# Reversing the k-steps of the middle token tile in the x-fed panels of a two-layer streaming encoder

## The chip, the cores and the metric

The kernel runs on one core of one Trainium2 chip. The metric is the device time of one execution, in microseconds (us). Before the change, three runs took 2115.74, 2115.85 and 2116.09 us, so the median is 2115.85 us. One further execution was profiled, and every row quoted here comes from it.

## The reference, cut to what matters

The model is one inference step of a two-layer encoder trunk over 1056 token rows (1024 of a prompt and 32 of a running stream), each with 1024 features. Each layer is a mixer and then a squared-ReLU MLP, with an RMS norm before and after each. In short:

```python
for l in range(2):
    hn = rmsnorm(x, norm_mix_pre[l])
    m = mixer_even(hn, ...) if l == 0 else mixer_odd(hn, ...)   # hn @ w_in first, w_out last
    x = x + rmsnorm(m, norm_mix_post[l])
    hn = rmsnorm(x, norm_ffn_pre[l])
    f = square(relu(hn @ mlp_up[l])) @ mlp_down[l]              # 1024 -> 4096 -> 1024
    x = x + rmsnorm(f, norm_ffn_post[l])
```

Four matrix products read the normed x: `w_in_even` (1024 to 2048 features), `mlp_up` of layer 0 (1024 to 4096), `c_w_in` (1024 to 3072) and `mlp_up` of layer 1. The change touches only these four. Each output feature is a sum over the 1024 input features. The kernel forms it in eight parts of 128, which are the k-steps, and they may be added in any order.

## The kernel before

**Data.** Features lie on the 128 partitions and tokens along the free dimension. The 1056 tokens are cut into three tiles of 352 columns, t = 0, 1, 2. Every fp32 operand of a product is kept as two rounded parts, high and low: `x_hi` and `x_lo` hold the normed x in eight feature chunks, and `h_hi` and `h_lo` hold the inner activations. A weight panel holds the 1024 x 128 weights of one output chunk, also as a high and a low part.

**Units.** `plan()` (line 79) writes down 736 units of TensorE work in the order in which they run. A whole unit is one panel times one tile. It consists of eight k-steps, and each k-step of three matmuls: weights high times data high (line 881), weights high times data low (line 882), and weights low times data high (line 883). That makes 24 matmuls of 352 columns into one PSUM bank. The first has `start`, the last has `stop` and increments the semaphore `pe_unit` (line 885). The bank is the unit's number modulo six. A unit that reads x is marked `src == "X"`. The 280 remaining units that are not whole are Strassen products of the MLP's down projection (lines 927 to 930), each with 12 matmuls of 264 columns.

**Phases.** `START` holds the first units of the four phases that read x: 0, 72, 356 and 452. The first twelve units of a phase are a block of four panels, tile by tile, and the semaphore `x_ready` is waited for only in units 0, 4 and 8 of a phase, once for each k-step (lines 875 and 876). After that block, a panel goes through its three tiles in a row: 0, 1, 2, or 2, 1, 0 for the third and fourth panel of a Strassen group's up projection (line 159). Phase 0 has 12 panels after its block, phases 1 and 3 have 28 each and phase 2 has 20.

**What sets the order around it.** `unit(n)` (line 863) waits once for all of its panel (`w_ready`, line 870) and once for its bank (line 871). It then issues the k-steps by `order`. `between(n, i)` (line 1060) inserts small matmuls after step number i of certain units, by position in the loop and not by k. The panels' transfers go out from SyncE (line 653), each after the last unit that reads the panel's slot (`pe_unit`). ScalarE makes the high part of the weights (line 1116). VectorE makes the low part and empties the banks after whole units (lines 1635 and 1678, for instance).

Of the kernel before, what the change touches and what calls it, by code (L numbers as in the profile page):

```python
# [205 lines left out]
def build(nc, A, O):  # L206
    UNITS, LOADS, START, OUT, GROUP = plan()
# [67 lines left out]
    with ExitStack() as ctx:  # L275
# [102 lines left out]
        def pt(buf, c, t):  # L378
            c0 = c * (buf.shape[1] // KC) + tile_at(buf, t)
            return buf[:, c0:c0 + TT]  # L380
# [36 lines left out]
        def w_k(l, which, k):  # L417
            v = W[l][which]
            if LOADS[l].slot in ("ha", "hb"):
                return v[:, k // 2, (k % 2) * P:(k % 2) * P + P]  # L420
            return v[:, k, :]
# [10 lines left out]
        def bank(n):  # L432
            return ps[:, R[n] % NB, 0:TT]
# [425 lines left out]
        def _(pe):  # L859
# [3 lines left out]
            def unit(n):  # L863
                u = UNITS[n]
                X = u.src == "X"
                src = (x_hi, x_lo) if X else (h_hi, h_lo)
                order = EVEN_ORDER if u.kind == "eo" else IN_ORDER[0:SC] if u.kind == "dn0" else IN_ORDER
                w0 = SC * (u.m % 2) if u.kind == "dn0" else 0
                l, t = u.load, u.t
                pe.wait_ge(w_ready, l + 1)  # L870
                bank_free(n)
                phase = START.index(max(s for s in START if s <= n))
                dst = bank(n)
                for i, k in enumerate(order):
                    if X and n - START[phase] in (0, 4, 8):
                        pe.wait_ge(x_ready, 24 * phase + 8 * t + k + 1)
                    if u.m == 0:
                        h_part(n, i)
                    hi, lo = pt(src[0], k, t), pt(src[1], k, t)
                    wh, wl = w_k(l, 0, w0 + k), w_k(l, 1, w0 + k)  # L880
                    nc.tensor.matmul(dst, wh, hi, start=(i == 0), stop=False)  # L881
                    nc.tensor.matmul(dst, wh, lo, start=False, stop=False)  # L882
                    last = nc.tensor.matmul(dst, wl, hi, start=False, stop=(i == len(order) - 1))  # L883
                    if i == len(order) - 1:
                        last.then_inc(pe_unit, 1)
                    between(n, i)

            def bank_free(n):
                o = bank_user[n]
                if o is not None:  # L890
                    pe.wait_ge(evac_a if UNITS[o].kind in SCALAR_OUT else evac_d, evac_no[o] + 1)
# [69 lines left out]
            def h_part(n, i):  # L961

                kind, t = UNITS[n].kind, UNITS[n].t
                if kind == "dn0" and i == 0:
                    pe.wait_ge(h_ready, index[n - 1 - t] + 1 - 8 + 4 * t)
                if kind == "dn3":
                    done = index[n - 1 - t] + 1
                    if i == 0 and t == 0:
                        pe.wait_ge(h_ready, done - 3)
                    if i == KC - 1:  # L970
                        pe.wait_ge(h_ready, done - 2 + t)
                if kind == "oo":
                    if i == 0 and t == 0:
                        pe.wait_ge(y_ready, 21)
                    if i == KC - 1:
                        pe.wait_ge(y_ready, 22 + t)
                if kind == "eo":
                    if i == 0 and t == 0:
                        pe.wait_ge(mix_a, 12)
                    if i == 4 and t == 0:  # L980
                        pe.wait_ge(mix_a, 21)
                    if i == KC - 1:
                        pe.wait_ge(mix_a, 22 + t)
# [76 lines left out]
            def between(n, i):  # L1060

                if n < START[1]:
                    if (n, i) in GATE_AT:
                        gate(*GATE_AT[n, i])
                    if (n, i) in VALUE_AT:
                        values_to_rows(*VALUE_AT[n, i])
                    if (n, i) in SPATIAL_AT:
                        spatial(SPATIAL_AT[n, i])
                if (n, i) in COL_AT:
                    col_sums(*COL_AT[n, i])  # L1070
# [10 lines left out]
            for n in range(4, N_UNITS):  # L1081
                if UNITS[n].kind in STRASSEN:
                    product(n)
                else:
                    unit(n)
# [7 lines left out]
            n = NORM[3, "post", 2]  # L1093
# [951 lines left out]
```

## Time and profile before

| what | value |
|---|---|
| median of three runs | 2115.85 us |
| the profiled execution's own time | 2116.21 us |
| its span, first to last instruction | 2114.1 us |
| mean granted TensorE clock | 0.999 of full |
| TensorE matmul busy | 2105.2 us, 100% |
| TensorE weight load busy | 2094.1 us, 99% |
| VectorE busy | 1187.2 us, 56% |
| ScalarE busy | 718.6 us, 34% |
| GpSimd busy | 279.3 us, 13% |

The profiled execution took 2.1 us more than its span. Busy time of matmuls is counted with overlap taken out, and each matmul's record is longer than the distance to the next one's start, so a busy TensorE is not one at its peak. For its pace one reads the distances between start times.

### The profile page before, as it was taken

What the parts mean: (1) busy time and instruction counts of PE and PEld (TensorE: products, weight loads), DVE (VectorE), ACT (ScalarE), POOL (GpSimd) and SP (SyncE); (2) the same over time, 40 slices, a digit from 0 to 9 for tenths busy, and PEclk for the clock granted to TensorE, in tenths of its full rate; (3) what the DMA queues carried; (4) which work ended last, traced back from release to release, by engine and by line L of the source; (5) the groups of instructions that cost most, each with busy time, mean ns of one, the idle gap of its engine ahead of it and who ended that gap; (6) DMA issues with size and microseconds to landing.
All of it is one profiled execution on the core that took longest, in us unless ns stands there. A gap on an engine that the chain in (4) does not pass through costs nothing.

```text
span 2114.1 us, 33629 instructions
## 1 busy us (share of the span) xinstructions
PE 2105.2 (100%) x13976; PEld 2094.1 (99%) x13976; DVE 1187.2 (56%) x1798; ACT 718.6 (34%) x1225; POOL 279.3 (13%) x307
## 2 busy tenths in 40 slices
PE   9999999999999999999999999999999999999998
PEld 9999999999999999999999999999999999999998
DVE  8766367364755747334953333384566475564336
ACT  6673345132232322333511112352313233232332
POOL 2000000031221312000033232000113022130000
PEclk9999999999999999999999999999999999999999
DMA  4111422111111111141311114131111111111142
GB/s 165 39 38 40 137 78 85 51 51 42 51 48 51 51 51 51 42 141 40 123 51 40 51 50 133 41 122 51 45 52 45 51 51 51 51 51 46 46 142 82
DMA packets 209189, 138.78 MB, mean 66 GB/s; under 512 B 6768, under 2 KB 205552, under 8 KB 209040
## 3 DMA queue, kind: packets, MB, share of 16 engines
q1 hardware_dynamic: 208320, 135.51, 21.1%
q8 instruction: 112, 1.84, 0.4%
q10 hardware_dynamic: 720, 1.13, 0.1%
q14 instruction: 37, 0.30, 0.0%
HBM read 119.22 MB, written 17.40 MB: 65 GB/s over the span
## 4 chain that ended last, share of the span: by engine, by line
PE 89%; issue 10%; DMA 0%; POOL 0%; DVE 0%; DVEq 0%; ACTq 0%; SPq 0%; POOLq 0%
PE ps L881 23%; PE ps L882 23%; PE ps L883 23%; PE ps L927 6%; PE ps L929 6%; PE ps L930 6%; PE ps L1003 1%; PE ps L1031 0%; PE ps L957 0%; PE ps L948 0%; DMA w_all_raw<-in_w_in_even_dram 0%; PE ps L944 0%; DMA w_all_raw<-in_mlp_down_dram 0%; PE ps L1014 0%; PE ps L990 0%
## 5 line engine op out<-in xcount | busy, mean ns | idle before, releaser
L881 PE MATMUL ps<-x_hi,w_all 128*128 128x352 f32 x2304 | 751.4, 326 | 0.0
L883 PE MATMUL ps<-x_hi,w_all 128*128 128x352 f32 x2304 | 739.4, 321 | 0.0
L882 PE MATMUL ps<-x_lo,w_all 128*128 128x352 f32 x2304 | 739.3, 321 | 0.0
L882 PEld LDWEIGHTS ps<-x_lo,w_all 128*128 128x128 f32 x2304 | 433.6, 188 | 2.2
L881 PEld LDWEIGHTS ps<-x_hi,w_all 128*128 128x128 f32 x2304 | 432.6, 188 | 2.7
L883 PEld LDWEIGHTS ps<-x_hi,w_all 128*128 128x128 f32 x2304 | 432.3, 188 | 0.0
L1116 ACT CAST w_all<-w_all_raw 128x1024 fp32r<-128x1024 f32 (+1 forms) x166 | 199.8, 1204 | 422.0 <-DMA w_all_raw<-in_mlp_up_dram 167.6
L927 PE MATMUL ps<-h_hi,w_all 128*128 128x264 f32 x1120 | 318.9, 285 | 0.0
L929 PE MATMUL ps<-h_lo,w_all 128*128 128x264 f32 x1120 | 318.6, 284 | 0.0
L930 PE MATMUL ps<-h_hi,w_all 128*128 128x264 f32 x1120 | 318.0, 284 | 0.0
L1635 DVE SCALAR_TENSOR_TENSOR tmp<-ps,rstd 128x352 f32<-128x352 f32 x192 | 100.1, 522 | 284.6 <-PE ps L883 284.5
L1643 DVE TENSOR_TENSOR f<-ps,f 128x528 f32<-128x528 f32 x280 | 195.7, 704 | 108.2 <-PE ps L930 107.8
L881 PE MATMUL ps<-h_hi,w_all 128*128 128x352 f32 x768 | 248.9, 324 | 0.0
L882 PE MATMUL ps<-h_lo,w_all 128*128 128x352 f32 x768 | 246.4, 321 | 0.0
L883 PE MATMUL ps<-h_hi,w_all 128*128 128x352 f32 x768 | 246.3, 321 | 0.0
L929 PEld LDWEIGHTS ps<-h_lo,w_all 128*128 128x128 f32 x1120 | 211.0, 188 | 0.0
L927 PEld LDWEIGHTS ps<-h_hi,w_all 128*128 128x128 f32 x1120 | 210.9, 188 | 0.0
L930 PEld LDWEIGHTS ps<-h_hi,w_all 128*128 128x128 f32 x1120 | 210.9, 188 | 0.0
L1466 DVE TENSOR_TENSOR w_all<-w_all_raw,w_all 128x1024 fp32r<-128x1024 f32 x126 | 153.8, 1221 | 17.6 <-ACT w_all L1116 17.6
L788 POOL TENSOR_TENSOR h_lo<-h_lo_raw,h_hi 128x528 fp32r<-128x528 f32 x20 | 26.5, 1325 | 972.7 <-ACT h_hi L1197 972.7
L881 PEld LDWEIGHTS ps<-h_hi,w_all 128*128 128x128 f32 x768 | 144.2, 188 | 0.3 <-DVE h_lo L1806 0.3
L882 PEld LDWEIGHTS ps<-h_lo,w_all 128*128 128x128 f32 x768 | 144.5, 188 | 0.0
(225 smaller groups left out, 2415.5 us busy)
## 6 DMA issues: line engine op xcount, KB each, us to landing
w_all_raw<-in_mlp_up_dram SPq DMA_DIRECT2D x60, 512.0 KB, 3.9
w_all_raw<-in_mlp_down_dram SPq DMA_DIRECT2D x96, 256.0 KB, 3.1
x_save<-f SPq DMA_DIRECT2D x9, 1408.0 KB, 6.5
x_old<-x_save SPq DMA_DIRECT2D x9, 1408.0 KB, 11.7
w_all_raw<-in_c_w_in_dram SPq DMA_DIRECT2D x22, 512.0 KB, 3.6
w_all_raw<-in_w_in_even_dram SPq DMA_DIRECT2D x12, 512.0 KB, 3.6
w_all_raw<-in_mlp_down_dram SPq DMA_DIRECT2D x12, 512.0 KB, 4.0
x_old<-in_x_cols_dram SPq DMA_DIRECT2D x3, 1408.0 KB, 11.2
```

The costliest lines, as they stand in the source:

```text
L788: nc.gpsimd.tensor_tensor(t_form(h_lo, 1, c), raw, t_form(h_hi, 1, c).bitcast(F32), ALU.subtract).then_inc(t1_ready, 1)
L881: nc.tensor.matmul(dst, wh, hi, start=(i == 0), stop=False)
L882: nc.tensor.matmul(dst, wh, lo, start=False, stop=False)
L883: last = nc.tensor.matmul(dst, wl, hi, start=False, stop=(i == len(order) - 1))
L927: nc.tensor.matmul(dst, wh, hi, start=(c == 0 and u.kind in CHAIN_START), stop=False, skip_group_check=True)
L929: nc.tensor.matmul(dst, wh, lo, start=False, stop=False, skip_group_check=True)
L930: last = nc.tensor.matmul(dst, wl, hi, start=False, stop=(c == 1), skip_group_check=True)
L1003: nc.tensor.matmul(ps[:, M0, 0:LT], gate_w[:, g, j, :], xc[j % 2][:, t * LT:(t + 1) * LT], start=True, stop=True).then_inc(gate_pe, 1)
L1116: nc.scalar.copy(W[l][0], W[l][2]).then_inc(w_high, 1)
L1466: nc.vector.tensor_tensor(lo, raw, hi.bitcast(F32), ALU.subtract).then_inc(w_ready, 1)
L1635: ins = nc.vector.scalar_tensor_tensor(sq_tmp(n)[:, :], bank(n), 0.0, scale, ALU.max, ALU.mult)
L1643: ins = nc.vector.tensor_tensor(sums, ps[:, a:a + 2, 0:QT], sums, ALU.add)
```

## The change

Inside `unit(n)`, for a unit that reads x, has t = 1 and is at least the thirteenth of its phase, the order of the eight k-steps is turned round: 7, 6, ... 0 in place of 0, 1, ... 7. The three matmuls inside a k-step keep their order. Nothing else is edited.

```diff
@@ -871,6 +871,8 @@
                 bank_free(n)
                 phase = START.index(max(s for s in START if s <= n))
                 dst = bank(n)
+                if X and t % 2 == 1 and n - START[phase] > 11:
+                    order = order[::-1]
                 for i, k in enumerate(order):
                     if X and n - START[phase] in (0, 4, 8):
                         pe.wait_ge(x_ready, 24 * phase + 8 * t + k + 1)
```

## Rows read from the trace of the kernel before

**Rows 1.** The page: its head, and busy time of each engine.

```profile
span 2114.1 us, 33629 instructions
PE 2105.2 (100%) x13976; PEld 2094.1 (99%) x13976; DVE 1187.2 (56%) x1798; ACT 718.6 (34%) x1225; POOL 279.3 (13%) x307
```

**Rows 2.** The page: 40 slices of the span, matmuls and granted clock, in tenths.

```profile
PE   9999999999999999999999999999999999999998
PEclk9999999999999999999999999999999999999999
```

**Rows 3.** Waits of TensorE matmuls (PE), then weight loads (PEld): us, times, longest us.

```profile
PE ps L1040 <- DVE rstd L1693: 1.3, 1, 1.3
PE ps L1048 <- ACT x_old L1453: 0.3, 1, 0.3
...
PEld ps L881 <- DVE h_lo L1806: 0.3, 1, 0.3
```

**Rows 4.** Line 881, by operands: count, duration ns min/median/max, first and last start.

```profile
L881 PEld LDWEIGHTS ps<-x_hi,w_all x2304: 186/188/193, 22.9 to 2009.5; 128*128 128x128 f32 x192
L881 PE MATMUL ps<-x_hi,w_all x2304: 317/323/597, 23.1 to 2009.7; 128*128 128x352 f32 x192
...
L881 PE MATMUL ps<-x_hi,h_hi x144: 320/323/409, 313.1 to 1430.5; 128*128 128x352 f32 x144
...
L881 PE MATMUL ps<-x_hi,w_s x16: 322/323/594, 34.8 to 56.0; 128*128 128x352 f32 x16
```

**Rows 5.** Timeline of matmuls, with the first of five units, after 492 us: start, duration (us).

```profile
492.37 0.28 PE L930 MATMUL ps<-h_hi,w_all 128*128 128x264 f32 x1
492.48 0.33 PE L881 MATMUL ps<-x_hi,w_all 128*128 128x352 f32 x1
...
496.36 0.32 PE L881 MATMUL ps<-x_hi,w_all 128*128 128x352 f32 x1
...
500.21 0.32 PE L881 MATMUL ps<-x_hi,w_all 128*128 128x352 f32 x1
...
511.49 0.32 PE L883 MATMUL ps<-x_hi,w_all 128*128 128x352 f32 x1
511.65 0.32 PE L881 MATMUL ps<-x_hi,w_all 128*128 128x352 f32 x1
511.81 0.32 PE L882 MATMUL ps<-x_lo,w_all 128*128 128x352 f32 x1
511.97 0.32 PE L883 MATMUL ps<-x_hi,w_all 128*128 128x352 f32 x1
...
515.47 0.32 PE L881 MATMUL ps<-x_hi,w_all 128*128 128x352 f32 x1
...
530.73 0.32 PE L881 MATMUL ps<-x_hi,w_all 128*128 128x352 f32 x1
```

**Rows 6.** Timeline of weight loads around 511.6 us: start, duration (us).

```profile
511.50 0.19 PEld L881 LDWEIGHTS ps<-x_hi,w_all 128*128 128x128 f32 x1
511.65 0.19 PEld L882 LDWEIGHTS ps<-x_lo,w_all 128*128 128x128 f32 x1
```

**Rows 7.** Two windows, Strassen products then x units: busy us and instructions of each engine.

```profile
455.00:490.00 35.00, 35.00 (x290) 35.00 (x289) 24.68 (x37) 6.42 (x6) 9.31 (x10) 1.00 0.16 46
500.20:538.35 38.15, 38.15 (x242) 38.15 (x241) 21.69 (x32) 16.06 (x32) 8.40 (x8) 1.00 0.15 42
```

**Rows 8.** Waits of VectorE and of SyncE's queue for TensorE: us, times, longest us.

```profile
DVE tmp L1635 <- PE ps L883: 284.5, 140, 3.3
...
SPq L669 <- PE ps L883: 803.7, 79, 17.5
```

## The prediction

> **What bounds the kernel.** I read the page's head first: the span is 2114.1 us and matmuls are busy for 2105.2 us of it [rows 1]. Then the slices, to see whether a stretch differs: all but the last have TensorE at nine tenths or more, and its clock is granted nearly in full throughout [rows 2]. Then the waits: in the whole execution TensorE's matmuls waited 1.6 us for other engines, once at the start and once in the tail, and the largest wait of a weight load at line 881 is 0.3 us [rows 3]. So no semaphore holds TensorE, and the kernel is a stream of 13976 matmuls. Its time can change only if the distance between the starts of two matmuls changes, if the number of matmuls changes, or if a new wait arises.
>
> The timeline gives that distance. The units that begin at 500.21 and 530.73 us are eight apart, so 192 matmuls took 30.52 us, 158.96 ns each [rows 5]. One unit of 24 matmuls takes 3.815 us. The records last 0.32 us, twice the distance, since a matmul's record goes on while the next has begun.
>
> **What the change removes, adds and moves.** It reverses the middle unit of each panel that comes after a phase's first twelve units: 12 panels in phase 0, 28 in phase 1, 20 in phase 2 and 28 in phase 3, together 88 units. That is 88 x 8 = 704 of the 2464 k-steps at line 881 that read x (2304 + 144 + 16, [rows 4]), and 88 x 24 = 2112 matmuls of 13976. No instruction goes or comes. What changes is which chunk of x and which block of weights a k-step reads. I take the possible costs one by one.
>
> *Waits on inputs.* The wait for `x_ready` stands only in units 0, 4 and 8 of a phase, and these are not reversed. By the thirteenth unit every chunk of every tile has been waited for. The wait for the weights covers a whole panel and was passed in the panel's first unit, which is never the middle one. So step 7, now first, needs nothing that is not there. Cost 0, covered by waits already passed.
>
> *Who waits for the unit.* VectorE empties a bank after the unit's last matmul; it waits 284.5 us in 140 cases at line 1635 for exactly that. SyncE's queue waits for the same count before a transfer, 803.7 us in 79 cases at line 669 [rows 8]. Both count whole units. The last matmul still stands at the end, whatever its k. No transfer starts earlier or later, and no queue is passed by a moved step: the k-steps issue no DMA. The small matmuls of phase 0 and the column sums are inserted by position. Cost 0. If a unit did end later, the cover is gone only for TensorE itself, and that is the case priced as the slow rival below.
>
> *Weight loads.* One could hope that a k-step which stays at k = 7 from tile 0 to tile 1, and at k = 0 from tile 1 to tile 2, saves a load. It would have to be of the same weights. But a k-step ends with the low weights (line 883) and the next begins with the high ones (line 881), so the two neighbours differ there too. And where neighbours do have equal weights, lines 881 and 882 in every k-step, the trace still has a load for each: 13976 loads for 13976 matmuls [rows 1], one at 511.50 and one at 511.65 us, 0.19 us each [rows 6]. The pair with equal weights is 0.16 us apart (511.65 to 511.81), and so is the pair with different ones (511.81 to 511.97) [rows 5]. So nothing is saved in the number of loads, and a saved load would show no gain in distance anyway. Value taken: 0.
>
> *The hops.* The reversal changes two kinds of steps from one matmul to the next. At the two edges of each reversed unit the hop becomes a stay on the same chunk, 2 x 88 = 176 hops. Inside it, a step up by one chunk becomes a step down by one, 7 x 88 = 616 hops. Together 792. The trace before has no step down by one, but it has larger ones: at each tile edge TensorE goes from chunk 7 back to chunk 0. The edge from tile 1 to 2 at 511.65 us is 0.16 us wide, as are its neighbours [rows 5]. Single distances are too coarse, so I compare whole units. From 500.21 to 515.47 us four units run through tiles 2, 0, 1, 2, that is with tile edges mostly upwards; it is 15.26 us. From 515.47 to 530.73 us four units run through tiles 2, 1, 0 and then 2 of the next panel, with edges downwards; it is 15.26 us again [rows 5]. The tile hop has changed direction and nothing is left of it at 0.01 us over four units, or 2.5 ns a unit. Put down to the two edges of a unit, that is 1.25 ns a hop. For 792 hops this bounds the cost to 792 x 1.25 = 1.0 us on either side. I take 0, since the nearest rows, the large backward hops, show no difference.
>
> *A wider bound from the pace itself.* A matmul's time has a part that follows its columns and a part that doesn't. In 35.00 us of Strassen products there are 290 matmul records of 264 columns, of which about two were in flight at the edge, so 35.00/288 = 121.5 ns each [rows 7]. Against 158.96 ns for 352 columns the slope is 37.4/88 = 0.425 ns a column. Of the 158.96 ns, 352 x 0.425 = 149.7 follow the columns and 9.3 are fixed. If hop or order were the cause of the fixed part, at most 2112 x 9.3 = 19.6 us could go. Against it speaks that the fixed part is the same whether the weights stay or change.
> The Trainium skill (TensorE: Matmul & The Clock Gate, section "Wait — 56ns, not 53.3ns?") gives the start-to-start distance at full clock as columns over 2.4 GHz plus about 2.5 ns. By that page alone it would be 149.2 ns here, an estimate. The trace disagrees: 158.96 ns. Were the reversed units to run at the page's pace, 2112 x 9.8 = 20.7 us would go. The page's rule has no term for the order of k, so it gives no reason why they should.
>
> **The sum.** Waits 0, loads 0, hops 0 with ends of -1.0 and +1.0 us. The profiled execution stays at a span of 2114.1 us and a time of 2116.2 us. That is 0.36 us above the median of the three runs, well within what one run differs from another (2115.74 to 2116.09 us). The forecast for the median is therefore 2115.85 us. About 0.2%, or 4.2 us, is what a measurement of this kernel can tell from no change.
>
> **The rivals.**
> *An edge that stays on a chunk is cheaper.* TensorE reads the same weight block and adjoining columns of x across the edge, and the whole fixed part of 9.3 ns goes at 176 hops: 1.6 us, 2114.2 us. For it: the operands are neighbours in memory. Against it: lines 881 and 882 share their weight block in every k-step and show no shorter distance [rows 5].
> *The fixed part goes in all of the reversed units.* 19.6 us, 2096.3 us. It needs a cause that sits in the direction of the steps inside a unit. For it is only that no row shows a step down by one; against it are the equal unit times for both directions of the tile edge.
> *Slower: reversed units lose the pace of the stream.* There is a slower pace in this trace: the units at 492.48 and 496.36 us, directly behind a Strassen group, take 3.88 and 3.85 us, not 3.815 [rows 5]. TensorE comes there from shorter matmuls, waits for nobody, and regains its pace in two units. If a step down by one chunk upset the fetching of operands ahead in the same way, each reversed unit would cost 0.065 us more, 88 x 0.065 = 5.7 us, or 2121.6 us. It decides from 4.2/88 = 0.048 us a unit, or 2 ns a matmul. Against it: the hops from chunk 7 to chunk 0, seven times as far, do not upset it from 500.21 us on.
> *The change doesn't act.* The reversed order is held in a name local to the unit and is read by the loop right after, so it acts on 88 units. Were it not to, the time would be the same 2115.85 us, and only the order of accumulation would tell.
>
> **How the numbers follow.** Forecast, no change beyond the hops' bound: 0.85. Cheaper edges: 0.07. No action: 0.01. Slow rival: 0.04. Fixed part gone in whole units: 0.03. The first three are within 0.2%, hence 0.93 for the same, 0.03 for faster and 0.04 for slower. The range holds the forecast with the hops' 1.0 us and the 0.4 us that medians may differ, and takes in the cheaper edges: 2114.2 to 2117.3 us. It leaves out the two far cases, 0.07 together.
>
> **What would show it.** In the profile after, the panels' middle units should again be 3.81 or 3.82 us long. The starts should stay at the same places within a tenth of a us to the end, with 13976 matmuls and as many loads, TensorE's waits at about 1.6 us in all, and the waits of VectorE and SyncE's queue for line 883 unchanged in count. The distance across a reversed unit's edges should be 0.16 us. The prediction is wrong if middle units are 0.05 us longer or shorter than the outer ones of the same panel, or if a wait appears before line 881. A change of the span with unchanged middle units would say that the cause is elsewhere and that I have overlooked something which counts k-steps.

## The result, and the profile after

The changed kernel takes 2125.70 us (median of four runs, 2125.50 to 2125.93) against 2115.87 us of the kernel before. The ratio is 1.0046, with a 95% interval of 1.0033 to 1.0059. No change was forecast, and 2114.2 to 2117.3 us as the range. The loss is 9.8 us.

The page's head of the kernel after, to be held against [rows 1]:

```profile
span 2123.9 us, 33629 instructions
PE 2115.1 (100%) x13976; PEld 2104.3 (99%) x13976; DVE 1187.8 (56%) x1798; ACT 718.8 (34%) x1225; POOL 279.4 (13%) x307
```

The counts are the same to the last instruction, and the span and the busy time of TensorE have grown alike, by 9.8 and 9.9 us. Next come the waits of the kernel after: TensorE's own, then VectorE's and that of SyncE's queue for TensorE (us, times, longest us). Line numbers behind the edit are two higher than before.

```profile
PE ps L1042 <- DVE rstd L1695: 1.3, 1, 1.3
PE ps L1050 <- ACT x_old L1455: 0.3, 1, 0.3
...
DVE tmp L1637 <- PE ps L885: 290.5, 140, 3.3
...
SPq L669 <- PE ps L885: 809.3, 79, 17.5
```

TensorE waits for the others for 1.6 us, as before [rows 3]. VectorE and SyncE's queue wait for TensorE as many times as before, and each about 6 us longer in all [rows 8]. So no wait has arisen. TensorE itself runs slower.

Where it does is seen in windows. The first two rows are the kernel before, the last two the kernel after. The columns are: window, its length, then busy us and instructions of PE, PEld, DVE, ACT and POOL, the granted clock, the DMA share and GB/s. The first window is TensorE's work on x panels in phase 2, the other on that phase's output panels.

```profile
1100.00:1290.00 190.00, 190.00 (x1197) 190.00 (x1196) 64.47 (x97) 25.02 (x46) 55.97 (x54) 1.00 0.16 46
1315.00:1380.00 65.00, 65.00 (x411) 65.00 (x411) 25.64 (x33) 26.04 (x48) 0.00 (x0) 1.00 0.25 76
```

```profile
1100.00:1290.00 190.00, 190.00 (x1181) 190.00 (x1180) 62.84 (x95) 26.23 (x49) 54.21 (x54) 1.00 0.16 46
1315.00:1380.00 65.00, 65.00 (x411) 65.00 (x410) 22.93 (x30) 22.44 (x41) 0.00 (x0) 1.00 0.26 85
```

In the same 190 us TensorE does 16 matmuls fewer, at a granted clock of 1.00 in both. (By the lengths of the units below it is 161.1 ns a matmul in place of 158.9; the windows' counts include matmuls cut by their ends.) The output panels, which read h in unchanged order, run at the old pace but for the first two units. This window of 190 us serves below as a yardstick: 1197 matmuls is the fast pace and 1181 the slow one.

Then the timeline of the kernel after, the first matmul of the same units as in [rows 5] (start, duration in us):

```profile
492.59 0.33 PE L883 MATMUL ps<-x_hi,w_all 128*128 128x352 f32 x1
...
496.47 0.33 PE L883 MATMUL ps<-x_hi,w_all 128*128 128x352 f32 x1
...
500.34 0.33 PE L883 MATMUL ps<-x_hi,w_all 128*128 128x352 f32 x1
...
515.80 0.33 PE L883 MATMUL ps<-x_hi,w_all 128*128 128x352 f32 x1
...
531.27 0.33 PE L883 MATMUL ps<-x_hi,w_all 128*128 128x352 f32 x1
```

Before, the first unit behind the Strassen group took 3.88 us, the second 3.85, and from 500.21 us on each took 3.815. After, they take 3.88 and 3.87, and from 500.34 us on it is (531.27 - 500.34)/8 = 3.866 us a unit to the end of the stretch. All three tiles are slow, not only the reversed one. Added up over the x units of phases 1 to 3 that come after a phase's first twelve, the middle tiles lost 3.1 us and the two untouched tiles 6.3 us. TensorE no longer leaves the slow pace that the trace before shows at 492.48 us. It leaves it only in the output panels, whose order is unchanged: behind phase 2 their first unit (at 1305.95 us) takes 3.87 us, the second 3.85 and the third 3.81. And where TensorE comes in fast, nothing is lost: the twelve x units from 405.94 us on take 3.813 us each. They follow units of only four k-steps, 24 in phase 1 and as many in phase 3, which the section on the kernel before counts as whole ones.

### The profile page after: what moved, and what is told of

Read it like the earlier page. It is cut to its first block, busy times and chain, and to the rows that moved or that the text cites. A ratio compares the mean times of both kernels' runs of the same rounds, so it can differ in the third digit from the quotient of the medians.

```text
span 2123.9 us, 33629 instructions
## 1 busy us (share of the span) xinstructions
PE 2115.1 (100%) x13976; PEld 2104.3 (99%) x13976; DVE 1187.8 (56%) x1798; ACT 718.8 (34%) x1225; POOL 279.4 (13%) x307
## 4 chain that ended last, share of the span: by engine, by line
PE 89%; issue 10%; DMA 0%; POOL 0%; DVE 0%; DVEq 0%; ACTq 0%; SPq 0%; POOLq 0%
PE ps L883 23%; PE ps L885 23%; PE ps L884 23%; PE ps L929 6%; PE ps L931 6%; PE ps L932 6%; PE ps L1005 1%; PE ps L1033 0%; PE ps L959 0%; DMA w_all_raw<-in_w_in_even_dram 0%; PE ps L950 0%; PE ps L946 0%; PE ps L1016 0%; DMA w_all_raw<-in_mlp_down_dram 0%; PE ps L992 0%
```

## The experiments

**The theory.** Chunk k of tile t begins (1056k + 352t) x 4 = 128 x (33k + 11t) bytes into x. Whether this is an even or an odd multiple of 128 bytes goes by k + t; call it the parity of a k-step. `x_lo` begins an even number of times 128 bytes behind `x_hi`, so it has the same parity. In steps of one chunk the parity alternates. Before, it was repeated at both edges of a middle unit: k=7,t=0 (odd) to k=0,t=1 (odd), and k=7,t=1 (even) to k=0,t=2 (even). The reversal makes these edges alternate as well. Theory A: a repeat of parity takes TensorE out of a slow pace, and pure alternation keeps it there. Theory B: steps down cost. Theory C: the same weight block on both sides of an edge costs.

**Order and parity apart.** Two kernels, each with one line in place of the change's:

```diff
-                    order = order[::-1]
+                    order = (6, 5, 4, 3, 2, 1, 0, 7)      # e1_down_even
+                    order = (1, 2, 3, 4, 5, 6, 7, 0)      # e2_up_odd
```

> Only the order of the reversed units is another: 6, 5, 4, 3, 2, 1, 0, 7 in all 88. Chunk k of tile t starts 128 x (33k + 11t) bytes into x, so whether it is an even or an odd multiple of 128 bytes goes by k + t (its parity). Before the change the two edges of a middle unit repeat a parity (k=7,t=0 to k=0,t=1, and k=7,t=1 to k=0,t=2); the full reversal lets the parity alternate everywhere. Theory A (the missing repeats leave TensorE in the slower of two paces, 161 instead of 159 ns a matmul): this order starts even and ends odd, so both edges repeat a parity again, hence 2115.9 us. Theory B (each step down by one chunk costs): six of seven inner steps go down still, 2115.9 + 9.8 x 6/7 = 2124.3 us. Theory C (the same weight block on both sides of an edge costs): no edge has it, 2115.9 us.

> The order of the 88 middle units is 1, 2, 3, 4, 5, 6, 7, 0: all steps go up but for the last. Theory A (parity repeats at the edges missing): it starts odd and ends even, no parity is repeated, 2125.7 us, and all three tiles of a panel at 3.867 us. Theory B (steps down cost): 2115.9 us, or 2117 with the single large one. Theory C (same weight block at an edge costs): the edge 7 to 1 is free of it and the edge 0 to 0 has it, half of 9.8 us, 2120.8 us.

The first took 2115.93 us (ratio 1.0000, 0.9991 to 1.0009), the second 2125.70 us (1.0047, 1.0032 to 1.0062). Six of seven steps down cost nothing where the edges repeat a parity. Steps up cost all of the 9.8 us where they don't. The yardstick window, first kernel and then second:

```profile
1100.00:1290.00 190.00, 190.00 (x1197) 190.00 (x1196) 64.48 (x97) 25.04 (x47) 56.04 (x54) 1.00 0.16 46
```

```profile
1100.00:1290.00 190.00, 190.00 (x1181) 190.00 (x1180) 62.86 (x95) 26.19 (x48) 54.09 (x54) 1.00 0.16 45
```

Theory B is refuted by both, theory C by the second, where it expected 2120.8 us.

**Which operand.** The change was applied to one operand alone:

```diff
+                    mid = X and t % 2 == 1 and n - START[phase] > 11
+                    kx = KC - 1 - k if mid else k            # e3_x_only
+                    hi, lo = pt(src[0], kx, t), pt(src[1], kx, t)
...
+                    kw = KC - 1 - k if mid else w0 + k       # e4_w_only
+                    wh, wl = w_k(l, 0, kw), w_k(l, 1, kw)
```

> In the 88 middle units only the chunk of x is reversed, the weight block goes 0 to 7, so the products pair the wrong chunks; number and size of all instructions are as before. Theory A (parity of the addresses of x): 2125.7 us. Theory B (steps down in x): 2125.7 us; if it is steps down in the weights, 2115.9 us. Theory C (same weight block at an edge): 2115.9 us.

> The counterpart: in the 88 middle units only the weight block is reversed, the chunk of x goes 0 to 7, so the products pair the wrong chunks. The blocks of a panel lie 512 bytes apart, so their parity never changes. Theory A (parity of the addresses of x): 2115.9 us. Theory B with steps down in the weights, and theory C: 2125.7 us.

With only x reversed it took 2125.60 us (1.0046, 1.0031 to 1.0061), with only the weights reversed 2115.82 us (1.0000, 0.9990 to 1.0009). It is the order of the addresses of x that matters, not that of the weight blocks. In both kernels the products pair the wrong chunks, so their time alone is used. The weight blocks of a panel are 512 bytes apart and never change parity.

**Does each reversed unit pay, or does the stretch keep a pace?**

```diff
-                if X and t % 2 == 1 and n - START[phase] > 11:
+                if X and t % 2 == 1 and n - START[phase] > 11 and u.m > 0:   # e5_down_later
                     order = order[::-1]
```

> The change as it was, but without the panels with m = 0 (74 units reversed in place of 88). These 14 are nearly all the first x panel behind a Strassen group or behind the phase's block, where TensorE arrives at its slow pace. Theory A with a memory (a pace is kept while the parity alternates, and each repeat of a parity moves TensorE one step from the slow to the fast one): the forward panel repairs the pace (3.879, 3.848, 3.812 us), the reversed ones behind it keep the fast one, 3.813 us a unit in place of 3.813, 3.815 and 3.818. 2115.9 less some 70 panels x 0.007 us = 2115.4 us. Theory A without a memory (each reversed unit pays at its own edges), and any theory in which a reversed unit costs by itself: 2115.9 + 9.8 x 74/88 = 2124.1 us.

It took 2115.48 us (five rounds, 2115.20 to 2115.95; before 2115.85 in the same rounds; ratio 0.9998, 0.9989 to 1.0007). 74 of 88 reversals cost nothing when a forward panel has come before them. The timeline of this kernel, first matmuls of the units as above:

```profile
492.14 0.33 PE L883 MATMUL ps<-x_hi,w_all 128*128 128x352 f32 x1
...
496.02 0.32 PE L883 MATMUL ps<-x_hi,w_all 128*128 128x352 f32 x1
...
499.87 0.32 PE L883 MATMUL ps<-x_hi,w_all 128*128 128x352 f32 x1
...
515.12 0.32 PE L883 MATMUL ps<-x_hi,w_all 128*128 128x352 f32 x1
...
530.37 0.32 PE L883 MATMUL ps<-x_hi,w_all 128*128 128x352 f32 x1
```

The first two units take 3.88 and 3.85 us as in the kernel before, and from 499.87 us on eight units take 30.50 us, 3.813 each. So alternation keeps the fast pace as well as it keeps the slow one.

**Many repeats.** All x units behind the first twelve of a phase took the even chunks first, then the odd ones:

```diff
+                if X and n - START[phase] > 11:
+                    order = (0, 2, 4, 6, 1, 3, 5, 7)      # e6_even_odd
```

> All three tiles of every x panel behind the first twelve units (264 units) take their k-steps as 0, 2, 4, 6, 1, 3, 5, 7: six parity repeats inside a unit. If alternation itself costs and a repeat saves time, the units get shorter than 3.813 us. If a repeat only moves TensorE out of the slow pace and costs 2 to 3 ns at the fast one (3.815 and 3.818 us in units with a repeat, against 3.813 without), it is 264 x 6 x 2.5 ns = 4 us more, 2119 to 2120 us. Theory B (steps down cost) has one step down a unit and expects 2116 us.

2117.39 us (1.0007, 0.9998 to 1.0016). A repeat is not fast by itself. The amount was overestimated: 1.5 us lost in place of 4. A panel of this kernel has 20 repeats and takes 3.820 us a unit in place of 3.813, about 1 ns a repeat and not 2.5. In this trace the first unit behind Strassen takes 3.93 us, and in its first four steps, whose parity is all even, the matmuls stay about 0.167 us apart. That fits what the slow units show inside. In the kernel after, 211 units without small matmuls, all with their weights in the three weight slots, take 3.87 us, and in them every k-step of even parity takes 0.490 us and every one of odd parity 0.476 or 0.477. At the fast pace, with alternating parity, all k-steps take 0.474 to 0.479 us. In e6 a unit at the fast pace takes 3.82 us with its repeats.

**A kick instead of the edges.** All 88 units stay reversed, and twelve first units of a stretch get two repeats inside:

```diff
                     order = order[::-1]
+                if X and (UNITS[n - 1].kind in STRASSEN or n in (START[0] + 12, START[2] + 12)):
+                    order = (0, 1, 3, 2, 4, 5, 6, 7)      # e7_down_kick
+                    order = (0, 1, 3, 2, 5, 4, 6, 7)      # e10_down_kick_apart, in its place
```

> The change as it was, all 88 units reversed, and in addition 12 forward units get the order 0, 1, 3, 2, 4, 5, 6, 7: the first x unit behind each Strassen group, the first behind the block of phase 2 and of phase 0. That order has two repeats (1 to 3, 2 to 4) inside the unit. Theory A with a memory: these twelve units bring TensorE to the fast pace and the reversals keep it there, 3.813 us a unit to the end of the stretch; the whole 9.8 us vanish and some 0.5 us more, about 2115 us. If repeats inside a unit, where the weight block changes parity in nothing, do not work as those at the edges do: 2125.7 us. Any theory in which reversed units cost by themselves: 2125.7 us.

It took 2120.26 us (1.0021, 1.0012 to 1.0029), half of the loss and between the two expectations. The timeline shows why: the second unit and all behind it take 3.84 us.

```profile
496.34 0.32 PE L885 MATMUL ps<-x_hi,w_all 128*128 128x352 f32 x1
...
500.18 0.32 PE L885 MATMUL ps<-x_hi,w_all 128*128 128x352 f32 x1
...
530.90 0.32 PE L885 MATMUL ps<-x_hi,w_all 128*128 128x352 f32 x1
```

From 500.18 to 530.90 us it is 3.840 us a unit. There are three paces, and alternation keeps each. The order had only taken TensorE one step.

Another version rests on the theory in its first form. It reverses only in phases 1 to 3 and has the same kick also in other slow units:

```diff
+                if X and t % 2 == 1 and n - START[phase] > 11 and phase > 0:
+                    order = order[::-1]
+                if X and (UNITS[n - 1].kind in STRASSEN or phase > 0 and n - START[phase] in (2, 10)):
+                    order = (0, 1, 3, 2, 4, 5, 6, 7)
+                if u.kind in ("oo", "dn3", "eo") and (u.m, t) == (5, 2):
+                    order = (4, 5, 7, 6, 0, 1, 2, 3) if u.kind == "eo" else (0, 1, 3, 2, 4, 5, 6, 7)
```

> A version built on theory A to beat both kernels: reversals in phases 1 to 3 only (76 units), the order with two repeats in the first x unit behind a Strassen group, in the third and eleventh unit of the blocks of phases 1 to 3 (3.869 and 3.877 us before, and slow ones behind them), and in the unit with m = 5, t = 2 of the four output blocks (3.867 us). Theory A with a memory: behind Strassen 10 x 0.07, alternation 70 x 0.007, blocks 3 x 0.25, outputs 4 x 0.05 us, together 2.1 us: 2113.8 us. Otherwise at least 2115.9 us, up to 2124.

It took 2119.67 us (1.0018, 1.0009 to 1.0026) and sat at the middle pace as well. In the next two kernels the two repeats are three steps apart. The second of them keeps the forward order where m = 0:

> All 88 units reversed, and the 12 first units with the order 0, 1, 3, 2, 5, 4, 6, 7 in place of 0, 1, 3, 2, 4, 5, 6, 7, which took 2120.3 us since 3.840 us a unit stayed for the whole stretch. If the second repeat had come too early: 3.813 us a unit, 2115 us. If an even repeat inside a unit does nothing at the middle pace: 2120.3 us again. If reversed units cost by themselves: no less than 2120.

```diff
-                    order = (0, 1, 3, 2, 4, 5, 6, 7)                    # e8_best
+                    order = (0, 1, 3, 2, 5, 4, 6, 7)                    # e9_both
...
-                    order = (4, 5, 7, 6, 0, 1, 2, 3) if u.kind == "eo" else (0, 1, 3, 2, 4, 5, 6, 7)
+                    order = (4, 5, 7, 6, 1, 0, 2, 3) if u.kind == "eo" else (0, 1, 3, 2, 5, 4, 6, 7)
```

> The version that reversed 74 units took 2115.48 us; this one reverses its 65 of phases 1 to 3, and gives the first x unit behind each Strassen group, the third and eleventh unit of three blocks and one unit of each output block the order 0, 1, 3, 2, 5, 4, 6, 7. Its two parity repeats (1 to 3, both odd, and 4 to 6, both even) stand three k-steps apart, not one as in 0, 1, 3, 2, 4, which left TensorE on a pace between the two (3.840 us a unit). Theory A with three paces, where a repeat of each parity is wanted with some k-steps between: fast behind each such unit, 2114.1 us (Strassen sites 10 x 0.05, blocks 3 x 0.15, outputs 4 x 0.07, alternation 0.5 us). If an even repeat inside a unit does nothing wherever it stands: blocks and outputs go to the middle pace, the two edges behind Strassen do the rest, 2115.0 us. Neither if theory A is wrong: 2116 us or more.

All 88 reversed with the kick apart: 2115.03 us (0.9996, 0.9987 to 1.0005), where 2115 was expected. The other: 2113.93 us (0.9991, 0.9983 to 1.0000), where 2114.1 was expected. The yardstick window of the kernel with all 88 reversed and the close kick, and of the same with the kick apart:

```profile
1100.00:1290.00 190.00, 190.00 (x1190) 190.00 (x1189) 63.93 (x96) 25.34 (x48) 55.09 (x52) 1.00 0.16 45
```

```profile
1100.00:1290.00 190.00, 190.00 (x1198) 190.00 (x1197) 64.45 (x97) 25.29 (x48) 56.05 (x54) 1.00 0.16 47
```

**Against what does the parity count?** Every weight slot was moved up by 128 bytes, and x was not (the small buffers behind the slots moved with them; the x units' matmuls read none of these):

```diff
-        at_byte[0] += 64
+        at_byte[0] += 192
         at_w = at_byte[0]
```

> The kernel before with its weight slots (and the small buffers behind them) 128 bytes further up, so that every weight block changes from an odd to an even multiple of 128 bytes against x, while x stays. All orders are those of before. It is the base for the next one. If the parity that counts is that of x against the weight block (loads and reads meet), odd and even repeats swap roles; the forward orders have both at the edges of a middle unit, so the pace is repaired in the same panel or one unit later: 2115.9 to 2117 us. If only x counts: 2115.9 us, unit by unit the same.

> All 88 units reversed with the order 0, 1, 3, 2, 5, 4, 6, 7 in the 12 first units (which took 2115.03 us), and the weight slots 128 bytes further up. If it is x against the weight block: the odd repeat, which comes first, now does what the even one did at the slow pace, nothing, and only the second works, so that 3.840 us a unit stay for the stretch: about 2120.3 us. If only the parity of x counts: 2115.0 us.

The forward kernel took 2114.13 us (0.9992, 0.9983 to 1.0002), below both expectations. The kernel with 88 reversals and the kick took 2113.44 us (0.9989, 0.9980 to 0.9998), and the expected 2120.3 us were wrong. The timeline of the forward kernel with moved slots gives the reason:

```profile
492.64 0.33 PE L881 MATMUL ps<-x_hi,w_all 128*128 128x352 f32 x1
...
496.46 0.32 PE L881 MATMUL ps<-x_hi,w_all 128*128 128x352 f32 x1
...
500.28 0.32 PE L881 MATMUL ps<-x_hi,w_all 128*128 128x352 f32 x1
```

The first unit behind Strassen takes 3.82 us in place of 3.88. The slow pace is not entered there, so there was nothing to mend. Of the 1.7 us that this kernel gained, about 0.9 lie in the Strassen products themselves. So the place of the weights against x matters, as far as the small buffers that moved too have no part in it.

The swap of roles shows in the same trace, in a stretch of phase 0 that is entered at the slow pace. These are the first matmuls of tiles 1, 2, 0, 1 and 2:

```profile
201.40 0.33 PE L881 MATMUL ps<-x_hi,w_all 128*128 128x352 f32 x1
...
205.27 0.32 PE L881 MATMUL ps<-x_hi,w_all 128*128 128x352 f32 x1
...
209.12 0.32 PE L881 MATMUL ps<-x_hi,w_all 128*128 128x352 f32 x1
...
212.96 0.32 PE L881 MATMUL ps<-x_hi,w_all 128*128 128x352 f32 x1
...
216.77 0.32 PE L881 MATMUL ps<-x_hi,w_all 128*128 128x352 f32 x1
```

The odd repeat before tile 1 leaves TensorE slow (3.877 us in the trace's ns, 3.87 by these rounded rows). The even one before tile 2 takes it to the middle pace (3.85, then 3.84), and the next odd one to the fast pace (3.81). In the layout as it was, the odd one came first with the step to the middle pace and the even one second with the step to the fast pace (492.48 to 500.21 us, [rows 5]). Inside the slow units the roles are swapped too: with the slots moved the odd k-steps take 0.490 us and the even ones 0.477.

Next the change itself was run where TensorE enters fast:

> The change exactly as it was, all 88 middle units reversed, with nothing else but the weight slots 128 bytes further up. With them there the forward kernel no longer came out of the Strassen groups at the slow pace (its first x unit took 3.818 us in place of 3.878) and ran 2114.13 us. Theory A with a memory (the alternation only keeps the pace it finds): the stretches behind Strassen and behind the block of phase 2 stay at 3.813 us a unit, a little better than forward (3.813, 3.818, 3.815): 2114.13 less 75 panels x 0.007 us = 2113.6 us. The same change then makes the kernel faster than with forward order. Only phase 0, which enters slowly (3.876 us), stays slow, up to 0.5 us more. Any theory by which reversed units or their edges cost by themselves: 2114.1 + 9.8 = 2123.9 us.

The change word for word, with the slots moved, took 2113.68 us (0.9989, 0.9980 to 0.9998): the reversal makes the kernel 9.8 us slower in one layout, and not slower, rather some 0.5 us faster, in the other (2114.13 us forward, which ran in other rounds). Its yardstick window:

```profile
1100.00:1290.00 190.00, 190.00 (x1198) 190.00 (x1197) 64.47 (x97) 25.30 (x48) 55.96 (x54) 1.00 0.16 48
```

Only the first stretch of phase 0 stays slow, three units of 3.867 us behind one with four small matmuls between its k-steps. This stretch doesn't keep to the theory. With the two repeats three steps apart and the odd one first, it stayed slow in the layout as it was (3.867 us) and was fast with the slots moved (3.813), the other way round from what the roles say. Perhaps small matmuls in between move the pace as well; that was not tested.

The last kernel gives another order to the remaining slow units:

```diff
+                if X and phase > 0 and n - START[phase] == 2:
+                    order = (0, 2, 1, 4, 3, 5, 6, 7)
+                if u.kind in ("oo", "dn3", "eo") and (u.m, t) == (5, 1):
+                    order = (4, 6, 5, 0, 7, 1, 2, 3) if u.kind == "eo" else (0, 2, 1, 4, 3, 5, 6, 7)
```

> As the other, and the units that were still slow with the weight slots moved (third unit of three blocks: 3.867 and 3.861 us; m = 5, t = 1 of the four output blocks and the one behind: 3.867 and 3.870 us) get an order with the even repeat first and the odd one three k-steps later: 0, 2, 1, 4, 3, 5, 6, 7. If odd and even have swapped their roles with the weights' address: 3 x 0.07 + 4 x 0.08 = 0.5 us less than the other, 2113.1 us. If the roles had not swapped: the same as the other or slower by up to 0.2 us, since those units would stop at the middle pace.

It took 2113.33 us (0.9988, 0.9979 to 0.9997), the best of all, 2.6 us below the kernel before in the same rounds. The third and fourth unit of phase 1, without that order and then with it:

```profile
321.38 0.32 PE L883 MATMUL ps<-x_hi,w_all 128*128 128x352 f32 x1
...
325.25 0.32 PE L883 MATMUL ps<-x_hi,w_all 128*128 128x352 f32 x1
...
329.11 0.32 PE L883 MATMUL ps<-x_hi,h_hi 128*128 128x352 f32 x1
```

```profile
321.47 0.32 PE L887 MATMUL ps<-x_hi,w_all 128*128 128x352 f32 x1
...
325.30 0.32 PE L887 MATMUL ps<-x_hi,w_all 128*128 128x352 f32 x1
...
329.12 0.32 PE L887 MATMUL ps<-x_hi,h_hi 128*128 128x352 f32 x1
```

They take 3.87 and 3.86 us without it, 3.83 and 3.82 with it: the even repeat first brings TensorE to the fast pace there. In the output blocks only the middle pace was reached (3.88 and 3.84 us in place of 3.87 and 3.87), so the gain was 0.35 us and not 0.5. The expectation had overlooked something there. The edited unit has t = 1, where an even k has odd parity. So the same order puts the odd repeat first (0 to 2) and the even one later (3 to 5). That makes these units the counter-test. With the slots moved an odd repeat first does nothing and only the even one works, as the swap of roles says. In the forward kernel with moved slots, too, units with an odd repeat at their front edge take 3.818 us and those with an even one 3.815, where it was 3.815 and 3.818 before.

## Why the prediction was wrong

*What bounds the kernel*, the count of 88 units and 2112 matmuls, the waits and their cover held. Nothing waits anew, and the counts of waits are the same.

*Weight loads* at no gain held. In the kernels with all 88 reversed and the repeats apart (e10) or the slots moved (e13) the same block stands on both sides of 176 edges, and their units take 3.813 us, as do those of the forward kernel that have no repeat in front of them.

*The hops* is the step that failed. It took the equality of two stretches of four units, with tile edges up and tile edges down, as the price of any other hop, and made 1.25 ns a hop and 1.0 us of it. Two things were wrong in that. First, all eight units lie in the fast pace, where even the full reversal costs nothing (3.813 us a unit in e5): the rows could not show what a hop does at the slow pace. Second, a hop has no price of its own here. The edges that the change removed had a function, to bring TensorE from 3.88 to 3.81 us behind every Strassen group and behind the block of phase 2. What was lost stands in the units that follow, two thirds of it in units that the change doesn't touch. The two units at 492.48 and 496.36 us were in the rows, and the question that they put, why the pace returns just at the tile edges, was not asked.

*The slow rival* named the right pace and the right place to read it (3.88 us, 0.065 us a unit), and got 0.04. Its mechanism was wrong: not steps down by one chunk (with six of the seven left it took 2115.93 us, with none left 2125.70 us), and not the reversed unit alone. Its 5.7 us counted 88 units at 0.065 us. It was rather 193 units at 0.05 on average, for all three tiles of a stretch stay slow. What spoke against it, that hops from chunk 7 to 0 don't upset the fast pace, was true and beside the point, for at the edges of a middle tile these hops, with the parity that they repeat, are the cure.

*What would show it* had the test that middle units be 0.05 us longer than the outer ones of their panel. It would have raised no alarm, since the outer ones became as slow. What shows the loss is the other sign that the prediction named, middle units of 3.81 or 3.82 us (they take 3.87), or the same units before.

The Trainium skill (TensorE: Matmul & The Clock Gate, section "Step-by-step: what each phase is for") has TensorE read its two operands from SBUF through two independent ports, one for the streamed operand and one for the weights. One could take from it that the weights' address has no bearing on how x is read; the page itself says nothing of addresses. The runs don't bear that reading out. The same program with its weight slots 128 bytes further up is 1.7 us faster in the median (2114.13 against 2115.78 us, with an interval that just includes no difference, though the slowest of its runs lies below the fastest of the kernel before), and the reversal costs 9.8 us in one layout and nothing in the other.

What stays open is the cause inside the chip. Shown are three paces, what leads from one to the next where no small matmuls come between, and that the layout of x against the weight slots enters. Why TensorE leaves the Strassen products slow in one layout, why the two repeats must be some steps apart, and whether the reads of the two operands meet somewhere in the memory, was not measured. The slots were moved by 128 bytes only. No run moved them by 256, which would leave the parity as it is, so that it is their parity that counts is the simplest reading and not shown. The small buffers behind the slots were not moved apart from them either.

## What to carry to other kernels

In a dense stream of matmuls the pace may have more than one stable value. Look in the trace for units of equal work whose lengths differ by one or two per cent, and ask what ends such a stretch before touching the order or the layout there. Before calling a reordering free, compute the byte addresses of both operands and compare the pattern of their parities (here of 128 bytes) before and after, above all at the seams between loops. Moving a buffer by 128 bytes is a cheap thing to try.

## What the runs showed of the hardware

With 352 columns and high and low parts, at a granted clock of 1.00 throughout, TensorE ran at three paces: 3.813, 3.840 and 3.867 us for 24 matmuls, that is 158.9, 160.0 and 161.1 ns each. Each lasted for whole stretches (the 190 us of the yardstick window and more) while the 128-byte parity of x alternated from one k-step to the next. Behind a Strassen group TensorE came in at the slow one with the weight slots as they were, and at the fast one with them moved by 128 bytes. In the first layout an odd repeat and, some steps later, an even one led to the fast pace. Which parity does what swapped with the slots moved. At the slow pace the k-steps of one parity took 490 ns and those of the other 477: the even ones were the long ones in the first layout, the odd ones in the second. At the fast pace a single repeat at a unit's front edge cost 1.5 or 5 ns (3.815 and 3.818 us against 3.813), and 20 in a panel about 1 ns each.
